# Attention scores at the head of each grouped step of a two-layer encoder

## The reference

```
h = rms_norm(x); proj = h @ w_in            # q/k/v of both kinds of heads
# 8 query heads of 64 over 2 key/value heads, rotary, both directions:
s = q @ k.T * 64**-0.5;  p = softmax(s);  o_g = p @ v
# 4 differential heads of two maps each:
p = softmax(s1) - lam * softmax(s2);      o_d = rms_norm(p @ v) * (1 - lam_init)
x = x + concat(o_g, o_d) @ w_out
gate, up = split(rms_norm(x) @ w_gate_up);  x = x + (silu(gate) * up) @ w_down
```

## Time and profile before

| what | value |
|---|---|
| time, median of 3 runs | 1812.74 us (1812.22 to 1813.41) |
| the profiled execution, its own time | 1814.41 us |
| its span in the profile | 1812.4 us |
| TensorE busy | 1760.7 us, 97% of the span |
| VectorE busy | 1183.6 us, 65% |
| ScalarE busy | 798.4 us, 44% |
| mean granted clock of TensorE | 0.994 of full speed |
| grouped steps, layer 0 | 184.75 to 257.60 us after the span's start |
| grouped steps, layer 1 | 1079.90 us to 1152.30 us |

### The profile page before, as it was taken

How to read it: one execution, slowest core, us unless ns; L and a number is a source line. 1 busy time by engine, 2 the same in 40 slices (tenths; PEclk the granted TensorE clock), 3 DMA queues, 4 the chain that set the end, 5 groups by cost and what they waited for, 6 DMA issues and landing times.

```text
span 1812.4 us, 28642 instructions
## 1 busy us (share of the span) xinstructions
PE 1760.7 (97%) x11280; PEld 1552.5 (86%) x11280; DVE 1183.6 (65%) x1959; ACT 798.4 (44%) x1772; POOL 268.6 (15%) x396
## 2 busy tenths in 40 slices
PE   6999999999999999999999999999899999999998
PEld 6888777778989899999888877777799898989896
DVE  5655888686756566666556468886877474756565
ACT  5233777644333333333333348775534242424242
POOL 3201435440000000000012015362400000000000
PEclk9999999999999999999999999999999999999999
DMA  5221000202222222221222110002022222222222
GB/s 173 63 66 47 25 2 25 71 1 82 71 70 70 70 69 72 60 80 47 70 70 59 59 36 25 2 25 71 31 74 70 70 71 62 69 62 68 67 81 82
DMA packets 121733, 108.20 MB, mean 60 GB/s; under 512 B 3361, under 2 KB 95649, under 8 KB 121601
## 3 DMA queue, kind: packets, MB, share of 16 engines
q1 hardware_dynamic: 120240, 101.79, 18.8%
q0 software_dynamic: 928, 3.02, 0.6%
q10 hardware_dynamic: 432, 1.57, 0.2%
HBM read 103.22 MB, written 3.15 MB: 59 GB/s over the span
## 4 chain that ended last, share of the span: by engine, by line
PE 69%; DVE 3%; ACT 2%; issue 1%; POOL 0%; POOLq 0%; ACTq 0%
PE bank L1707 11%; PE bank L2029 11%; PE bank L2033 11%; PE bank L2031 11%; PE bank L1709 10%; PE bank L1708 10%; PE bank L1801 2%; PE bank L1792 1%; DVE neg_max L1381 1%; PE bank L1949 1%; PE bank L1748 0%; POOL hrstd L620 0%; PE bank L1787 0%; ACT stage L974 0%; PE bank L1725 0%
## 5 line engine op out<-in xcount | busy, mean ns | idle before, releaser
L1707 PE MATMUL bank<-w_hi,hT_hi 128*128 128x512 f32 (+1 forms) x624 | 245.3, 393 | 9.9 <-DVE x L1493 9.3
L1709 PE MATMUL bank<-w_hi,hT_lo 128*128 128x512 f32 (+1 forms) x624 | 234.4, 376 | 0.0
L1708 PE MATMUL bank<-w_lo,hT_hi 128*128 128x512 f32 (+1 forms) x624 | 233.8, 375 | 0.0
L618 POOL TENSOR_TENSOR ms<-ss,eps_col 128x1 f32<-128x1 f32 x30 | 6.6, 220 | 1053.4 <-ACT headsq L813 1053.4
L1275 DVE TENSOR_TENSOR x<-x,bank 128x512 f32<-128x512 f32 x120 | 81.2, 686 | 118.8 <-PE bank L1709 118.2
L1707 PEld LDWEIGHTS bank<-w_hi,hT_hi 128*128 128x128 f32 x624 | 118.0, 189 | 43.2 <-DVE x L1493 11.5
L1709 PEld LDWEIGHTS bank<-w_hi,hT_lo 128*128 128x128 f32 x624 | 117.9, 189 | 21.9
L1708 PEld LDWEIGHTS bank<-w_lo,hT_hi 128*128 128x128 f32 x624 | 118.3, 190 | 17.0
L2029 PE MATMUL bank<-hT_hi,w_hi 128*128 128x384 f32 x368 | 123.5, 336 | 0.7 <-issue 0.7
L2033 PE MATMUL bank<-hT_hi,w_lo 128*128 128x384 f32 x368 | 123.6, 336 | 0.0
L1801 PEld LDWEIGHTS bank<-v,stage 128*128 128x128 f16 x2400 | 106.5, 99 | 19.7 <-issue 9.6
(11 more groups left out here) (214 smaller groups left out, 4601.0 us busy)
## 6 DMA issues: line engine op xcount, KB each, us to landing
x_raw<-in_w_gate_up_dram SPq DMA_DIRECT2D x44, 512.0 KB, 5.0
w_raw<-in_w_gate_up_dram SPq DMA_DIRECT2D x44, 512.0 KB, 4.0
w_raw<-in_w_in_dram SPq DMA_DIRECT2D x36, 512.0 KB, 3.7
w_raw<-in_w_down_dram SPq DMA_DIRECT2D x36, 512.0 KB, 3.8
w_raw<-in_w_out_dram SPq DMA_DIRECT2D x16, 512.0 KB, 3.7
x_raw<-in_w_down_dram SPq DMA_DIRECT2D x8, 512.0 KB, 3.7
out_dram<-stage SPq DMA_DIRECT2D x6, 512.0 KB, 2.6
gain<-in_gains_dram POOLq DMA_DIRECT2D x4, 512.0 KB, 3.9
```

Source lines behind the costliest of these rows:

```text
L1707: pe.matmul(out, a_hi, b_hi, start=first, stop=False)
L1708: pe.matmul(out, a_hi, b_lo, start=False, stop=False)
L1709: return pe.matmul(out, a_lo, b_hi, start=False, stop=last)
```

## The change

The call of `scores` moves from the third place of a grouped step to the first. It carries its waits along: the step now begins with the wait for both exps of step e, where it began with the wait for the first one. The other engines' code is the same.

```
@@ -1822,10 +1822,10 @@
             def grouped_step(l, e):
 
                 p, t = divmod(e, T)
+                scores(l, e + 2, {4: p * 2 + 2, 0: p * 2 + 1}.get(t))
                 gqa_transpose(l, e, t, 0)
                 if mixed_at(e):
                     transpose_mix(l, *mixed_at(e), True)
-                scores(l, e + 2, {4: p * 2 + 2, 0: p * 2 + 1}.get(t))
                 if e:
                     grouped_product(l, e - 1, 1)
                 gqa_transpose(l, e, t, 1)
```

## The result

The changed kernel takes 1843.51 us (1841.63 to 1846.83, five runs) against 1812.74: a ratio of 1.0168 [1.0157, 1.018], 30.8 us slower by the medians. Its profiled execution took 1841.63 us, the shortest of the five, with a span of 1839.7; the forecast was 1841.4 for the profiled execution and 1840 for the median.

What follows compares the result with a forecast made beforehand. TensorE was taken to set the grouped stage's pace (busy 16.86 of 17 us). Six later pairs (21.8) plus two first pairs (5.2) gave 27.0 us: 1841.4 profiled, 1840 median; own range 1836 to 1845, widened to 1829 to 1851.

Steps and rivals of the forecast that it cites:

- The mechanism: Grouped steps: scores moved ahead no longer cover the transposes-to-product stretch, so product 0 idles; 1.5 us of cover against 2.05.
- The way, 2.05 us: First head's transposes through ScalarE and VectorE to their product, read bare at the stage's end: 0.67 + 0.63 + 0.75 us.
- The first pair, 2.6: First pair of heads in each layer: t = 2 to 5 cost 2.31 plus 0.3 for the cold start, twice 5.2 us.
- the 0.3 taken: Start of each layer's stage: allowance for the two cold steps and the second exp's wait, bounds 0 and 1 us.
- All else stays: Everything outside the grouped stage was to keep its time; no change in us.
- TensorE's busy time stays: Whole program: nothing is added or removed, so TensorE's busy time was to stay the same.
- The median: Median of the runs, from the profiled execution's 1841.4 us less the 1.7 it lay above the median: about 1839.7, 1840.
- that rival: Idling in every grouped step also lowers TensorE's clock: 1862 us, 1851 if half hides in waits, near 1888 throughout; chance 0.08.
- the rule named there: Skill's account of a kernel whose TensorE idles briefly and often, its clock swinging; would favour one clock fall per pair, 1862.
- The stretch at 396 us: Argument against a clock fall: between 396 and 398 us TensorE is busy 0.77 of 2 us at granted clock 1.00.
- Faster: Grouped stage: earlier scores make row maxima and exps ready sooner and remove 6.4 us of TensorE waits: 1806; chance 0.03.
- No change: Grouped steps: new idle stretches replace waits elsewhere, or the chip's order stays as it was: about 1813; chance 0.03.

Runs made afterwards that it cites:

- a shorter way: Changed kernel, VectorE making head 0's low half for only the first half of the keys in grouped steps: 1838.3 us; same cut in the kernel before: 1810.38.
- steps changed apart: Two kernels against the one before: scores first only at t = 4 and 5, 1824.47 us; scores first only at t = 0 to 3, 1835.22 us.
- tile and exp on both sides: Unused 4-byte tile and early one-column exp for layer 1 added to the kernel before, 1801.34 us, and to the changed kernel, 1831.31 us.
- the kernel before with half of the low half: Kernel before, low half of head 0's transposed probabilities made for the first half of the keys only, high half used for the rest: 1810.38 us.

## Why the prediction was right, step by step

- **The mechanism** (scores ahead of the way, not beside it): right. Each product 0 idles; with a shorter way the changed pair shrinks by 0.7 us and the old one by 0.2; and the prices of steps changed apart add up to the whole within 0.2 us a pair.
- **The way, 2.05 us**: too small by 0.1, since it was taken from a product with one wait left, and product 0 has two. That is +0.09 in each of t = 2, 4 and 5. The exps at t = 0 and 1 came 0.06 sooner than worked out. A middle pair is 21.09 against 20.88, and the six later pairs cost 23.2 against 21.8.
- **The first pair, 2.6**: too small in this execution. To the scores of step 8 it costs 3.4 and 3.6 us (layer 0: 179.24 to 207.94, where before it was 179.25 to 204.56). The start and the two cold steps together cost 0.46 for the second exp and 0.02 (192.80 - 185.21 = 7.59 against 7.57): 0.48 against the 0.3 taken. The third step was costed at full clock; its scores ran partly at half of it, 0.6 more. But the low clock falls elsewhere in other executions: with tile and exp on both sides the first pair costs 2.7 and 2.0 (28.77 against 26.05 us in layer 0, 28.08 against 26.06 in layer 1). So the term can't be held to better than 2.0 to 3.6.
- **All else stays**: in the two profiled executions wrong by 2.9 us, which came back outside the stage. So the stage lost 30.2 against 27.0 forecast, and the two errors nearly cancel in the span. That is luck: the 2.9 come and go between executions, whatever the order of the scores (1652.5 to 1655.5 us outside the stages in nine kernels with the same tiles and the same end of the stage). What gives them was not tried.
- **TensorE's busy time stays**: it grew by 5.9 us. Rows that follow each other at once overlap, and ahead of a wait the whole row counts as busy, so part of the waiting stands without a bracket: product 1 at 202.42 comes 0.71 after the transposes at 201.71, whose row takes 0.66; at 205.60 it comes only 0.50 after them.
- **The median**: the profiled execution came out as worked out (1841.63 against 1841.4), by the luck just told. The step from it to the median failed: the profiled run lay 1.7 above the median before, and 1.9 below it after. By the medians the change costs 30.8 us, 3.5 more than the 27.3 of the forecast; the six later pairs explain 1.4 of that.
- **The rivals**: the clock stayed at 1.00 in the later pairs of both layers although TensorE idles in each step, so that rival fell, and with it, for this kernel, the rule named there from the Trainium skill ("TensorE: Matmul & The Clock Gate", section "A second HAM failure mode: psum-queue depth-cycling"): 17.81 of 21 us busy, at 1.00. The stretch at 396 us was a weaker argument than it looked: behind the same stretch in the changed kernel the granted clock is 0.50 at 413 to 415 us, and in the kernel before with half of the low half at 400 to 402. Faster: the waits of the first steps grew from 3.5 to 4.4 us instead of going, and those for a low half from 2.9 to 25.7. No change: each idle stretch came on top of the old time.

## What to carry to other kernels

In a queue that is worked off in order, independent work is worth most between a producer and the consumer of what other engines make of it: measure that way where the trace shows it bare, subtract what still stands beside it, and each step costs the difference. Take the bare way from an instruction with the same waits as the one that will wait, and give the steps after a cold start a range, since the place of the low clock differs from one execution to the next. Compare variants with the same tiles: a tile that is allotted and not used can move the time by a third of what this change did.

## What the runs showed of the hardware

- The unused tile of 4 bytes per partition: 10.7 us, 0.6% of the time, most of it in matmuls outside the grouped stages, by up to 2% each (396 to 389 ns).
- A product whose queue had one more wait ahead of it started 0.15 us after the data instead of 0.06, although the other wait had long been met.
- The low clock at a stage's start (1.2 GHz) set in 6.1 to 9.0 us after the layer's first scores in kernels that have the same instructions up to there, and in one layer of one run it did not come; which instructions it hits decides 0.5 to 0.7 us of a step.
